# A two-layer trunk kernel on one Trainium2 core: another order of loads and work at the kernel's beginning, and one step moved in each layer's mixer

## The reference

```python
for l in range(DEPTH):
    h = rmsnorm(x, attn_norm[l])
    x = x + hybrid_mixer(h, ...)      # proj = h @ w_in; branches A gMLP, B block attention,
                                      # C latent attention, D convolution; sigmoid gates; w_out
    h = rmsnorm(x, ffn_norm[l])
    x = x + (swiglu(h, ...) if l % 2 == 0 else moe_swiglu(h, ...))

def rmsnorm(x, g):
    xf = x.astype(jnp.float32)
    y = xf * lax.rsqrt(jnp.mean(xf * xf, axis=-1, keepdims=True) + NORM_EPS)
    return (y * g.astype(jnp.float32)).astype(x.dtype)
```

## Time and profile before

| | |
|---|---|
| median of 3 runs | 1110.23 us (1107.61 to 1112.32) |
| the profiled execution | 1109.89 us, span 1108.1 us |
| TensorE busy | 97% of the span |
| VectorE, ScalarE, GpSimd busy | 76%, 59%, 3% |
| mean granted clock of TensorE | 0.99 |
| DMA | 248.66 MB, 224 GB/s over the span |

### The profile page before, as it was taken

How to read it: one execution, slowest core, us unless ns; L and a number is a source line. 1 busy time by engine, 2 the same in 40 slices (tenths; PEclk the granted TensorE clock), 3 DMA queues, 4 the chain that set the end, 5 groups by cost and what they waited for, 6 DMA issues and landing times.

```text
span 1108.1 us, 15999 instructions
## 1 busy us (share of the span) xinstructions
PE 1070.7 (97%) x5740; PEld 917.9 (83%) x5740; DVE 838.9 (76%) x1178; ACT 650.0 (59%) x907; POOL 28.4 (3%) x76
## 2 busy tenths in 40 slices
PE   6999999999999999989999989999999999999997
PEld 6977888888999997878888877878787888888885
DVE  4789887654545447799887666898989898989895
ACT  4757655453434435658555456576766666766763
POOL 6000000030000000000000000000000000000000
PEclk9999999999999999999999999999999999999998
DMA  9625454665456454435455555989898989898981
GB/s 271 215 95 179 157 170 164 234 177 190 158 184 196 168 204 159 145 107 174 157 183 174 175 205 191 331 293 355 288 355 291 357 289 353 291 355 287 360 289 49
DMA packets 125325, 248.66 MB, mean 224 GB/s; under 512 B 4912, under 2 KB 50034, under 8 KB 125280
## 3 DMA queue, kind: packets, MB, share of 16 engines
q1 hardware_dynamic: 123136, 243.02, 64.1%
q0 software_dynamic: 2144, 5.03, 1.9%
HBM read 246.99 MB, written 1.05 MB: 224 GB/s over the span
## 4 chain that ended last, share of the span: by engine, by line
PE 83%; DVE 10%; ACT 4%; issue 2%; POOL 0%; ACTq 0%; DVEq 0%; POOLq 0%
PE bank L349 25%; PE bank L351 24%; PE bank L350 24%; DVE wlo L337 5%; ACT whi L330 2%; PE bank L908 1%; PE bank L907 1%; PE bank L966 1%; DVE h L1368 1%; PE bank L523 1%; PE bank L928 1%; PE bank L929 1%; DVE x L1366 1%; PE bank L617 0%; PE bank L607 0%
## 5 line engine op out<-in xcount | busy, mean ns | idle before, releaser
L337 DVE TENSOR_TENSOR wlo<-ring,whi 128x1024 fp32r<-128x1024 f32 (+2 forms) x506 | 541.2, 1121 | 98.5 <-ACT whi L330 97.6
L349 PE MATMUL bank<-whi,hTh 128*128 128x512 f32 (+3 forms) x1328 | 478.8, 361 | 10.1 <-DVE wlo L337 8.2
L330 ACT CAST whi<-ring 128x1024 fp32r<-128x1024 f32 (+2 forms) x506 | 457.1, 972 | 26.9 <-PE bank L351 16.0
L351 PE MATMUL bank<-whi,hTl 128*128 128x512 f32 (+3 forms) x1328 | 469.3, 353 | 0.0
L350 PE MATMUL bank<-wlo,hTh 128*128 128x512 f32 (+3 forms) x1328 | 468.8, 353 | 0.0
L349 PEld LDWEIGHTS bank<-whi,hTh 128*128 128x128 f32 x1328 | 252.0, 190 | 50.8 <-DVE wlo L337 15.8
L351 PEld LDWEIGHTS bank<-whi,hTl 128*128 128x128 f32 x1328 | 251.6, 189 | 30.5
L350 PEld LDWEIGHTS bank<-wlo,hTh 128*128 128x128 f32 x1328 | 252.1, 190 | 28.5 <-issue 0.5
L1696 DVE SCALAR_TENSOR_TENSOR act<-bank,rstd,sig 128x256 f32<-128x256 f32 x22 | 9.6, 479 | 57.9 <-ACT sig L1222 57.9
L349 PE MATMUL bank<-whi,oTh 128*128 128x512 f32 x128 | 51.9, 405 | 0.0
L351 PE MATMUL bank<-whi,oTl 128*128 128x512 f32 x128 | 50.6, 395 | 0.0
(11 more groups left out here) (300 smaller groups left out, 901.4 us busy)
## 6 DMA issues: line engine op xcount, KB each, us to landing
ring<-in_w_in SPq DMA_DIRECT2D x40, 1024.0 KB, 5.2
ring<-in_moe_w_down SPq DMA_DIRECT2D x40, 1024.0 KB, 5.7
ring<-in_moe_w_gate SPq DMA_DIRECT2D x32, 1024.0 KB, 7.8
ring<-in_moe_w_up SPq DMA_DIRECT2D x32, 1024.0 KB, 7.3
ring<-in_moe_w_gate SPq DMA_DIRECT2D x16, 768.0 KB, 5.5
ring<-in_moe_w_up SPq DMA_DIRECT2D x16, 768.0 KB, 4.4
ring<-in_ffn_w_gate SPq DMA_DIRECT2D x11, 1024.0 KB, 5.3
ring<-in_ffn_w_up SPq DMA_DIRECT2D x11, 1024.0 KB, 5.6
```

Source lines behind the costliest of these rows:

```text
L330: nc.scalar.copy(whi[pc.part(hf)][:, 0:n], pc.raw[:, hf * n:(hf + 1) * n]).then_inc(hi_done, 1)
L337: nc.vector.tensor_tensor(wlo[q][:, 0:n], pc.raw[:, hf * n:(hf + 1) * n], whi[q][:, 0:n].bitcast(F32), ALU.subtract).then_inc(lo_done, 1)
L349: nc.tensor.matmul(o, sh, wh, start=start, stop=False)
L351: return nc.tensor.matmul(o, sl, wh, start=False, stop=stop)
```

## The change

The norm row of layer 0 is loaded by SP between the two halves of x, under a semaphore of its own (`gain0_in`), no longer by GpSimd. GpSimd waits for piece 0 to land before it issues the parameters. At the beginning alone (k = 0) h is worked on in the order (0,0), (1,0), (0,1), (1,1), that is, first the column half 0 of both token halves; ScalarE and VectorE put piece 0 between the two column halves. TensorE's idle products there are 4 and 6 in place of 12 and 10. ScalarE does one tiny copy at `const_ready`. In both layers `prep` moves behind piece 3 on TensorE (behind `d_zT`) and on VectorE (behind the split of piece 5), and gMLP's lower part moves on VectorE to s = 9, ahead of the split of piece 11. The tiles `oTh` and `oTl` move out of the shared region, and the FFN's `aTh`, `aTl` and the router's `htokh`, `htokl` become views of them.

```diff
+def h_order(k):
+    return [(m, g) for g in range(2) for m in range(MT)] if k == 0 else [(m, g) for m in range(MT) for g in range(2)]
+
+def h_count(k, m, g):
+    return 4 * k + h_order(k).index((m, g)) + 1
...
-        aTh = [place(f"aTh{i}", [P, 2, T], F32R) for i in range(2)]
-        aTl = [place(f"aTl{i}", [P, 2, T], F32R) for i in range(2)]
+        aTh, aTl = ([t[:, i, :, :] for i in range(2)] for t in (oTh, oTl))
...
-            for m in range(MT):
-                sp.dma_start(x[:, m, :], a['x'][0, P * m:P * (m + 1), :]).then_inc(x_in[m], 16)
+            sp.dma_start(x[:, 0, :], a['x'][0, 0:P, :]).then_inc(x_in[0], 16)
+            sp.dma_start(gain[:, :], a['attn_norm'][0:1, :].to_broadcast([P, D])).then_inc(gain0_in, 16)
+            sp.dma_start(x[:, 1, :], a['x'][0, P:2 * P, :]).then_inc(x_in[1], 16)
...
-            load_gain(0)
...
+            pool.wait_ge(raw_in[Piece(0).slot], Piece(0).landed)
             load_params(0)
...
                 def small(s):
-                    if s == 2:
-                        prep(l)
                     if s == 3:
                         d_zT(l)
+                        prep(l)
...
             pe.wait_ge(const_ready, 1)
-            idle_products(12)
+            idle_products(4)
             transposed_h(0)
-            idle_products(10)
+            idle_products(6)
...
                 if k == 0:
                     norm_upper(k, 0)
+                    split_hi(act_e, Piece(0), piece_half(0))
                     norm_upper(k, 1)
-                    split_hi(act_e, Piece(0), piece_half(0))
                     split_hi(act_e, Piece(1), piece_half(1))
...
             act_e.wait_ge(const_ready, 1)
+            nc.scalar.copy(stat[:, 63:64], eps[:, :])
             token_norm(0)
...
-                lower_hT(k)
                 if k == 0:
+                    lower_hT(k, (0,))
                     split_lo(dve, Piece(0), piece_half(0))
+                    lower_hT(k, (1,))
                     split_lo(dve, Piece(1), piece_half(1))
...
                     if s == 9:
                         c_rotate_qk(l)
+                        o_lower(l, 0, 6)
                     if s + 2 < MIX_PIECES:
                         split_lo(dve, pcs[s + 2], piece_half(s + 2))
...
                     if s == 2:
                         glu(l)
+                    if s == 3:
                         prep(l)
...
                     if s == 10:
-                        o_lower(l, 0, 6)
                         b_sum_qk(l)
                         b_rotate_qk(l)
```

More of the change, by code:

```diff
@@ L132, in build_trunk @@
         hTl = place("hTl", [P, KD, T], F32R)
+        oTh = place("oTh", [P, NB, 2, T], F32R)
+        oTl = place("oTl", [P, NB, 2, T], F32R)
         ring = [place(f"ring{i}", [P, PIECE]) for i in range(RING)]
@@ L167, in build_trunk @@
         qkT = place("qkT", [P, 2, HEADS, T])
-        oTh = place("oTh", [P, NB, 2, T], F32R)
-        oTl = place("oTl", [P, NB, 2, T], F32R)
         zpad = place("zpad", [P, 2, D_CONV - 1 + T])
@@ L192, in build_trunk @@
         eact = act[:, :, :].rearrange("p m n -> p (m n)")
-        aTh = [place(f"aTh{i}", [P, 2, T], F32R) for i in range(2)]
-        aTl = [place(f"aTl{i}", [P, 2, T], F32R) for i in range(2)]
+        aTh, aTl = ([t[:, i, :, :] for i in range(2)] for t in (oTh, oTl))
         ering = ring + [place(f"ring{i}", [P, PIECE]) for i in range(RING, ERING)]
-        htokh = place("htokh", [P, MT, D], F32R)
-        htokl = place("htokl", [P, MT, D], F32R)
+        htokh, htokl = (t[:, :, :, :].rearrange("p n k t -> p (n k t)").rearrange("p (m d) -> p m d", d=D)
+                        for t in (oTh, oTl))
         xgh, xgl = (t[:, 0:4, :].rearrange("p k t -> p (k t)").rearrange("p (k t) -> p k t", t=P) for t in (hTh, hTl))
@@ L525, in transposed_h @@
             def transposed_h(k):
-                for m in range(MT):
-                    for g in range(2):
-                        pe.wait_ge(h_ready, 4 * k + 2 * m + g + 1)
-                        for j in range(4):
-                            last = nc.tensor.transpose(bank[h_bank(k, m, g)][:, P * j:P * (j + 1)],
-                                                       hm[:, m, P * (4 * g + j):P * (4 * g + j + 1)], ident[:, :])
-                        last.then_inc(hT_mm, 1)
+                for m, g in h_order(k):
+                    pe.wait_ge(h_ready, h_count(k, m, g))
+                    for j in range(4):
+                        last = nc.tensor.transpose(bank[h_bank(k, m, g)][:, P * j:P * (j + 1)],
+                                                   hm[:, m, P * (4 * g + j):P * (4 * g + j + 1)], ident[:, :])
+                    last.then_inc(hT_mm, 1)
             def prep(l):
@@ L1026, in square_sum, with norm_upper @@
                 return nc.scalar.activation(ym[:, m, :], x[:, m, :], ACT.Square, accum_out=ssum[:, m:m + 1])
-            def norm_upper(k, m):
-                for g in range(2):
-                    act_e.wait_ge(hT_mm, 4 * k + 2 * m + g + 1)
+            def norm_upper(k, part):
+                for m, g in h_order(k)[2 * part:2 * part + 2]:
+                    act_e.wait_ge(hT_mm, h_count(k, m, g))
                     nc.scalar.copy(hTh[:, 4 * g:4 * g + 4, P * m:P * (m + 1)],
@@ L1339, in _, with lower_hT @@
             V = nc.vector
-            def lower_hT(k):
-                for g in range(2):
+            def lower_hT(k, groups=(0, 1)):
+                for g in groups:
                     for m in range(MT):
-                        dve.wait_ge(hT_hi, 4 * k + 2 * m + g + 1)
+                        dve.wait_ge(hT_hi, h_count(k, m, g))
                         o = slice(P * m, P * (m + 1))
@@ L1351, in token_norm @@
             def token_norm(k, last_piece=None, stage=0, piece=None):
[L1354 to L1356 removed]
+                if k == 0:
+                    dve.wait_ge(gain0_in, 16)
+                    for m, c in h_order(0):
                         dve.wait_ge(x_in[m], 16)
[L1358 to L1365 removed]
+                        cols = slice(512 * c, 512 * (c + 1))
+                        V.tensor_tensor(hm[:, m, cols], x[:, m, cols], gain[:, cols], ALU.mult).then_inc(h_ready, 1)
+                else:
+                    dve.wait_ge(gain_in, 16 * k)
+                    for m in range(MT):
+                        if m == 0:
+                            dve.wait_ge(m0_done, stage)
+                        else:
+                            dve.wait_ge(w_used, 2 * last_piece.number + 2)
+                        for c in range(2):
+                            cols = slice(512 * c, 512 * (c + 1))
+                            o = x[:, m, cols]
                             V.tensor_tensor(o, o, bank[sum_bank(k, m, c)][:, :], ALU.add).then_inc(x_new, 1)
                             dve.wait_ge(x_new, 4 * (k - 1) + 2 * m + c + 1)
[L1368 removed]
+                            V.tensor_tensor(hm[:, m, cols], o, gain[:, cols], ALU.mult).then_inc(h_ready, 1)
                 V.engine_nop().then_inc(gain_free, 2)
[L1371 removed]
                 if k == 0:
+                    lower_hT(k, (0,))
                     split_lo(dve, Piece(0), piece_half(0))
+                    lower_hT(k, (1,))
                     split_lo(dve, Piece(1), piece_half(1))
[L1375 removed]
+                else:
+                    lower_hT(k)
+                if 0 < k < 3:
                     split_lo(dve, piece, piece_half(1) if k == 2 else HALF)
```

17 lines of the change are left out of this document (2 added, 15 removed).

## The result

The changed kernel took **1099.11 us** (median of 4 runs, 1097.11 to 1099.78), the kernel before 1110.18 (1107.61 to 1112.32); the ratio is 0.9898, 95% interval 0.9879 to 0.9918. The forecast was 1097.6. The total is near the forecast; what it is made of is not.

A forecast was written before the change was run, and what follows sets the result against it. TensorE, busy 97% of the span, bounds the kernel, so only its idle or low-clock time can be won. 6.9 us (start) plus 5.6 (low part) gives 12.5 off about 1110, so 1097.6 us; own range 1095.5 to 1099.5.

The forecast's parts named there:

- Norm row and supply of pieces 0 and 1: Start, SP queue: norm row lands at 5.5 us, x half 1 at 6.7, piece 0 at 9.6, piece 1 at 12.9.
- Two marks that were set: Signs at the start: norm row and x half 1 landed by 7 us, piece 0 by 10.
- First product: TensorE's first real product starts between 12.0 and 13.2 us, taken as 12.4, 5.7 us earlier than 18.06.
- Clock at the start: TensorE's clock rises ahead of the first real product; loss taken as 0.4 us, bounds 0 to 3.6.
- the rival: Start: clock stays low, 9 to 18 matmuls at 0.43 us, piece 2 at 26.0 to 27.8, time 1099.7 to 1101.5; chance 0.20.
- Function table: ScalarE at the start: a tiny copy at 5.3 us loads the table early, taking 1.28 us out of the path.
- Piece 2 at 23.8: TensorE starts the third weight piece at 23.8 us instead of 30.66, a gain of 6.9 us.
- The same work, one piece later: cost nothing: Preparation transposes move behind piece 3, at 32.1 us against parameters landing at 29.9: slack 2.2 us, no cost.
- The rival of the late parameters: Small loads start 3.9 us later, run against pieces 1 to 4 and stop the preparation transposes; slower than before; chance 0.02.
- Low part, 5.6: gMLP's lower part ahead of piece 11's split removes TensorE's key-transpose wait: 2.8 us per layer, bounds 2.5 to 3.0.
- The placement, costed at nothing: Low tiles' new place in memory, with aTh and htokh as views of oTh, changes no instruction or wait: no cost.
- wrong if TensorE waits for a piece between 24 and 60 us: Sign set against the forecast: TensorE waiting for a weight piece between 24 and 60 us would show it wrong.

The follow-up runs named there:

- kernel with three groups: Changed kernel with the parameter loads issued in three groups, behind pieces 0, 6 and 8, instead of all behind piece 0: 1093.74 us, ratio 0.9855.
- kernel with the fill: Changed kernel with 12 idle products on TensorE ahead of layer 0's z transposes, before piece 4: 1094.77 us, ratio 0.9867 of the kernel before.

## Why the prediction was right, and where it was not

- **Norm row and supply of pieces 0 and 1: right.** The row landed at 6.2 (5.5 forecast; it took 5.0 us from issue), x half 1 at 7.7 (6.7), piece 0 at 10.6 and piece 1 at 13.3 (9.6 and 12.9). x half 0 came at 4.2, as forecast, so the start-up was counted right; the row landed 2.0 us behind it and not 1.2, x half 1 1.5 behind the row, and what follows carries this. Two marks that were set, x half 1 by 7 and piece 0 by 10, were missed by 0.6 to 0.7 us.
- **First product: right, at the late end.** 13.04 against 12.0 to 13.2. Piece 0's landing decided it: its cast begins at 10.60, the lower part at 11.67. The second multiplication waited 0.77 for x, as worked out.
- **Clock at the start: the forecast, not the rival.** The clock rose at 9.96, during the transposes: from 0.21 us from start to start they go to 0.11, the idle products behind them are 0.11 apart, and the first product ran at full pace. The 0.4 us set aside for it were not spent. The page "TensorE: Matmul & The Clock Gate" of the Trainium skill (Part 4: PE-mode transpose) says that transposes don't count as busy in the same way, by which the clock would rise only behind the later products. The trace of the changed kernel, with its rise at the eleventh transpose, speaks against it; the kernel without the first idle products neither confirms nor refutes it.
- **Function table: right.** The load stands at 0.79 with 1.28 us, out of the path and even earlier than the 5.3 forecast. No drain shows beside it, nor beside the load at 12.00 before, so 1.28 us and not 2.66 is what stood in the path.
- **Piece 2 at 23.8: right** (24.05). The step held; that its 6.9 us would last to the end was wrong, for the next reason.
- **"The same work, one piece later: cost nothing": this is the step that failed.** The preparation was costed against its parameters' landing alone, 29.9 against 32.1; they landed at 27.6, earlier still. What wasn't followed was the z transposes' own input: dxc on VectorE, queued behind the split of piece 4, and so on piece 4's landing. And piece 4's landing was never worked out; the sum ended at piece 2. The rival of the late parameters even says that they now run against pieces 1 to 4, but it looked only for a loss at the preparation. The price was 5.5 us (kernel with three groups): 2.8 of wait and about 2.7 of clock (kernel with the fill).
- **Low part, 5.6: right in mechanism and size** (5.9 in the full change, 6.0 alone). Nothing was given back at the scores, so the upper bound, 3.0 per layer, is what came.
- **The placement, costed at nothing: wrong, 3.3 us.** "Changes no instruction and no wait" is true and says nothing of how fast an instruction goes.
- **The total** came out 1.5 us from the forecast by luck: a gain of 3.3 that was not seen stood in for most of a loss of 6.0 (6.9 - 0.9). The upper end of the forecast's own range doesn't come out of its terms either: 5.2 for the start (piece 2 at 25.5) and 5.0 for the layers give 1099.7, and 1100.7 with the 1 us for the clock, not 1099.5. The mark that was set, "wrong if TensorE waits for a piece between 24 and 60 us", was met by the wait that hung on piece 4. The range held, the reasoning for its larger term did not.

## What to carry to other kernels

When a start is pulled forward, follow the supply as far as the gain is meant to last: every load that was in flight in the old gap now flies beside later pieces, and the first consumer that is late may be behind a second engine's queue. Hold back loads until their user is near, in groups, and see whether a small step that is ready stands behind a split that isn't. When tiles are moved in memory, compare the spacing of the instructions that read them, even if the program is otherwise the same.

## What the hardware showed that was not expected

- Loads on GpSimd's queue take their full part of the 16 DMA engines from a large load on SP's. With 17 loads of 1.4 MB, the router's and a norm row of 0.5 MB about, a 1 MB piece took 13.0 us from its issue and not 5.8 to 6.4; moved, they took piece 6 from 6.1 to 14.1, and piece 1 from 10.6 to 18.2. How the two queues share is not shown beyond the bytes that each moved.
- The same 128x512 product starts 227 or 232 to 235 ns after the last, by where its stationary tile lies, with 32 bytes making the difference. With the moving tile 64 bytes further on it is 229, and the same 128x256 product starts 113 to 114 ns after the last, not 120.
- TensorE's clock fell to 1.2 GHz for 3.4 or 6.8 us in or shortly behind waits of 2.8 to 3.2 us in four of the five kernels that had one at the z transposes, and not in the fifth. Over all traces 7 of the 13 such waits, those at the key transposes among them, were followed by a fall. Medians moved by up to 3 us through such stretches far from the edit, so the local gain was read from the start times of like instructions, not from the medians.
